# A mixture-of-experts block with streamed weights: the experts that need two passes move from places 6, 12, 18, 24 to places 3, 10, 17, 24

## The reference

```python
logits = (xt @ router_w + router_b).astype(jnp.float32)
top_v, top_e = lax.top_k(logits, TOP_K)          # TOP_K = 4, N_EXPERTS = 32
wts = jax.nn.softmax(top_v, axis=-1)
...
def expert_block(args):
    xb, e = args
    hgu = xb @ w_gate_up[e] + b_gate_up[e]       # 1024 -> 2048
    gate, up = jnp.split(hgu, 2, axis=-1)
    gate = jnp.minimum(gate, SWIGLU_LIMIT)
    up = jnp.clip(up, -SWIGLU_LIMIT, SWIGLU_LIMIT)
    act = (up + 1.0) * (gate * jax.nn.sigmoid(SWIGLU_ALPHA * gate))
    return act @ w_down[e] + b_down[e]           # 1024 -> 1024
```

## Time and profile before

| | |
|---|---|
| three runs | 1380.29, 1381.20, 1381.88 us; median 1381.2 us |
| the profiled execution | 1381.2 us, of which its span is 1379.5 us |
| PE busy | 1339.8 us (97% of the span) |
| POOL busy | 710.9 us (52%) |
| DVE, ACT busy | 412.0 us (30%), 234.7 us (17%) |
| read from memory | 483.44 MB, mean 352 GB/s |
| expert stage | first block's `gate_up` ends at 434.87 us, the last block's at 1354.10 us |

### The profile page before, as it was taken

One profiled execution on the slowest core, in us unless ns is written; L12 is line 12 of the kernel. 1 busy time (PEld: TensorE's weight loads), 2 busy tenths in 40 slices (PEclk: granted clock), 3 DMA queues, 4 the chain that ended last, 5 costly groups with the idle time before them and its releaser, 6 DMA issues.

```text
span 1379.5 us, 17459 instructions
## 1 busy us (share of the span) xinstructions
PE 1339.8 (97%) x6442; PEld 624.2 (45%) x6443; DVE 412.0 (30%) x755; ACT 234.7 (17%) x401; POOL 710.9 (52%) x425
## 2 busy tenths in 40 slices
PE   5999999999999999999999999999999999999996
PEld 2888545788743333333333333333333333333332
DVE  2160015355664331113321322312232231231222
ACT  2320004310023111111211211211211211211202
POOL 0000000000013777768777677777677776777773
PEclk9899999999999999999999999999999999999999
DMA  9735342599757999999999989999899998999995
GB/s 351 252 123 183 122 138 106 190 324 362 275 227 308 431 428 429 429 399 420 428 429 429 427 365 428 430 427 429 363 429 429 427 429 362 430 429 427 431 427 221
DMA packets 70914, 485.89 MB, mean 352 GB/s; under 512 B 7254, under 2 KB 7418, under 8 KB 45450
## 3 DMA queue, kind: packets, MB, share of 16 engines
q1 hardware_dynamic: 69490, 480.56, 85.1%
q0 software_dynamic: 1056, 3.93, 1.0%
q10 hardware_dynamic: 344, 1.07, 0.2%
HBM read 483.44 MB, written 2.10 MB: 352 GB/s over the span
## 4 chain that ended last, share of the span: by engine, by line
PE 70%; DMA 26%; DVE 1%; issue 1%; POOL 1%; SPq 1%; ACT 1%; DVEq 0%; POOLq 0%; ACTq 0%
PE bank L1600 22%; DMA landing<-in_w_gate_up 17%; PE bank L1261 15%; PE bank L1647 12%; DMA landing<-in_w_down 7%; PE bank L1270 6%; PE bank L1579 4%; PE bank L1617 2%; PE bank L1496 2%; DMA piece<-in_w_ada 1%; PE bank L1634 1%; PE bank L1544 1%; POOL gu_slot L527 1%; PE bank L1607 1%; PE bank L1630 1%
## 5 line engine op out<-in xcount | busy, mean ns | idle before, releaser
L527 POOL COPY gu_slot<-landing 128x2048 f32<-128x2048 f32 x248 | 463.0, 1898 | 196.7 <-issue 117.5
L1600 PE MATMUL bank<-gu_slot,xg 128*64 128x512 f32 x2304 | 510.7, 593 | 8.8 <-POOL gu_slot L527 7.9
L1600 PEld LDWEIGHTS bank<-gu_slot,xg 128*64 128x64 f32 x2304 | 162.4, 137 | 329.0 <-issue 295.8
L527 POOL COPY dn_slot<-landing 128x2048 f32<-128x2048 f32 x124 | 231.3, 1897 | 76.3 <-issue 55.5
L1647 PE MATMUL bank<-dn_slot,actT 128*64 128x512 f32 x1152 | 255.1, 595 | 0.0
L1647 PEld LDWEIGHTS bank<-dn_slot,actT 128*64 128x64 f32 x1152 | 79.5, 137 | 171.2 <-issue 171.2
L1261 PE MATMUL bank<-hT,piece 128*128 128x256 f32 x704 | 155.1, 382 | 0.0
L1170 DVE TENSOR_SCALAR bank<-bank 128x512 f32<-128x512 f32 x36 | 25.2, 699 | 399.2 <-PE bank L1600 399.2
L1261 PEld LDWEIGHTS bank<-hT,piece 128*128 128x128 f32 x704 | 134.5, 192 | 19.6 <-issue 1.1
L744 ACT ACTIVATE sig<-bank 128x512 f32<-128x512 f32 x36 | 21.5, 598 | 696.7 <-PE bank L1600 696.7
L1180 DVE TENSOR_TENSOR ysb<-bank,gt2q 128x512 f32<-128x512 f32 x36 | 24.9, 692 | 253.7 <-PE bank L1647 253.7
(11 more groups left out here) (323 smaller groups left out, 902.7 us busy)
## 6 DMA issues: line engine op xcount, KB each, us to landing
landing<-in_w_gate_up SPq DMA_DIRECT2D x124, 2048.0 KB, 10.7
landing<-in_w_down SPq DMA_DIRECT2D x62, 2048.0 KB, 10.7
piece<-in_w_in SPq DMA_DIRECT2D x17, 2048.0 KB, 8.7
piece<-in_w_ada SPq DMA_DIRECT2D x12, 2048.0 KB, 13.1
gu_slot<-in_w_gate_up SPq DMA_DIRECT2D x8, 1024.0 KB, 7.3
piece<-in_w_branch_a SPq DMA_DIRECT2D x2, 2048.0 KB, 9.2
dn_slot<-in_w_down SPq DMA_DIRECT2D x4, 1024.0 KB, 11.3
piece<-in_w_branch_b SPq DMA_DIRECT2D x2, 2048.0 KB, 8.7
```

Of the source, the lines that this page charges most:

```text
L527: nc.gpsimd.tensor_copy(place, landing[j // 2 % 3][:, j % 2, :]).then_inc(there, 16)
L1600: ins = M(gu_bank[u][64 * q:64 * q + 64, :], xg[:, k % 4, 64 * (k // 4):64 * (k // 4) + 64], gu_slot[k][:, cols_], start=(k == 0), stop=(k ...
```

## The change

It is one table, written by GpSimd in the first stage. Ranks 0 to 4 now stand at places 3, 10, 17, 24, 31; ranks 5 to 8 at 7, 14, 21, 28; 9 to 12 at 5, 12, 19, 26; 13 to 17 at 1, 8, 15, 22, 29; 18 to 22 at 2, 9, 16, 23, 30; 23 to 26 at 4, 11, 18, 25; 27 to 30 at 6, 13, 20, 27; rank 31 at 0. With these inputs the four doubles are at 3, 10, 17 and 24.

```diff
             at = 0
-            for first, n in ((6, 5), (3, 5), (5, 5), (2, 5), (1, 6), (4, 5), (0, 1)):
+            for first, n in ((3, 5), (7, 4), (5, 4), (1, 5), (2, 5), (4, 4), (6, 4), (0, 1)):
                 step.settle()
-                step(nc.gpsimd.iota(place_of[:, at:at + n], [[6, n]], base=first, channel_multiplier=0,
+                step(nc.gpsimd.iota(place_of[:, at:at + n], [[7, n]], base=first, channel_multiplier=0,
                                     allow_small_or_imprecise_dtypes=True), numbers_ready if first == 0 else None)
                 at += n
```

## The result

The changed kernel took 1367.73 us (median of 4 executions, 1366.56 to 1368.81) against 1381.43 us for the kernel before (median of 4, 1380.29 to 1381.88): ratio 0.9902, 95% interval 0.9885 to 0.9919. It is 13.7 us faster where 9.2 were forecast, and 1367.73 lies under the range. The profiled execution of the changed kernel took 1366.56 us with a span of 1364.9 us, 14.6 us less than the span before.

A forecast was written before the change was run, and what follows sets the result against it. Weight transfers were taken to bound the expert stage until about 600 us, TensorE after. Removed waits (-10.40) and new ones (+1.27) gave -9.1 us, the queue's side -9.5 to -10.0; with -9.2 taken, 1381.2 became 1372.0 us, range 1370.0 to 1374.5.

The forecast's parts named there:

- The first double at 3: Expert stage: a second block at place 3 builds lead for the transfers, removing the waits of places 4 to 6, -10.40 us.
- The last double: End of the expert stage: it stays at place 24, seven singles and the tail follow, nothing changes but its time.
- Six singles between doubles: Expert stage: six singles outlast the lead slightly, so places 10, 17 and 24 newly wait 0.42 us each, +1.27 us.
- The 0.42: Lateness in us of place 31 before the change, taken as the wait into places 10, 17, 24 and 31 after it.
- The check from the queue's side: SyncE's issue queue: holds behind doubles fall from 18.1 or 17.6 us to 8.1, moving the end by -10.0 or -9.5 us.
- L = 20.4 us: Expert stage: the transfers' capped lead at the place behind a double; each single uses 3.47 us, so it lasts six singles.
- A lead that is shorter behind a double met with nothing in hand: Rival, expert stage: places 9, 16 and 23 wait too, at most 3.47 us more per stretch; 1375.5 to 1382.5 us; chance 0.06.
- A shortage of buffers: Rival, places 4 to 6: three landing buffers, not transfer rate, cause the pauses, which stay; 1382.5 us, no difference; chance 0.04.
- The clock in the expert stage: Rival: TensorE without pauses from 513 us drops its clock, about 7 us per stretch; two stretches give 1386 us; chance 0.03.
- The table does what it says: Answers a rival: if doubles were not ranks 0 to 3, they would not move to 3, 10, 17; no difference; chance 0.02.
- 1381.2 - 9.2: Whole kernel: profiled execution, also the median of three runs, less the gain taken from both sums, giving 1372.0 us.
- a rival in the other direction: The slower case: TensorE's clock falls after 513 us as in the first 100 us, about 7 us per stretch; chance 0.03.

The follow-up runs named there:

- e1: Kernel before with its same placement, table written in eight pieces instead of seven: 1378.61 us against 1377.45, ratio 1.0.
- e5: Kernel before plus 16 products of constants in TensorE's pauses at the start: 1378.1 us, ratio 1.0002 to the kernel before.
- e3: Against the kernel before: first double at place 3, steps kept at six (doubles at 3, 9, 15, 21): 1378.2 us, ratio 1.0005.
- e4: Against the changed kernel: first double back at place 6, steps of seven (doubles at 6, 13, 20, 27): 1378.4 us, ratio 1.0011 to the kernel before.
- e7: Against the changed kernel: steps of eight (doubles at 3, 11, 19, 27): 1378.97 us against 1377.73 for the kernel before, ratio 1.0004.
- e8: Against the changed kernel: first double at place 2, steps of seven (doubles at 2, 9, 16, 23): 1370.62 us, ratio 0.9955 to the kernel before.
- e2: The changed kernel timed again with no edit: 1367.48 us against 1377.45 for the kernel before, ratio 0.9924.
- e10: The changed kernel timed once more with no edit, beside the one with ten added products: 1366.88 us, ratio 0.9923 to the kernel before.
- e6: Changed kernel plus 16 products of constants in TensorE's pauses at the start: 1368.4 us, ratio 0.9933 to the kernel before.
- e9: Changed kernel plus ten products of constants at the start, none behind colA: 1369.33 us against 1377.62 for the kernel before, ratio 0.9948.

## Why the prediction was right and wrong

**The mechanism and the size of the gain in the expert stage: right.** The first double at 3 takes the 10.40 us of places 4 to 6 (measured: all three at 25.93). The step "The last double" was right too. The term "Six singles between doubles" was sized at 3 x 0.42 = 1.27 us and measured 0.24 + 0.23 + 0.11 = 0.58, and place 31 waits 0.28 instead of 0.42; place 3 is met 0.09 later. That is 10.40 - 0.58 + 0.14 - 0.09 = 9.87, and the trace shows 9.83. The 0.42 was one reading: with the same table place 31 is 0.19 late in e1 and 0.17 in e5, and in the five traces of the changed table the waits run from 0.06 to 0.38. The check from the queue's side, -9.5 to -10.0, was the better of the two sums. L = 20.4 us, drawn from one wait of 0.42, stood up to every placement: with it, and with the changed kernel's measured stage as the base, e3, e4, e7 and e8 were forecast at 919, 919.4, 919.6 and 911.9 us and came at 919.15, 919.56, 919.92 and 911.83.

**The rivals.** A lead that is shorter behind a double met with nothing in hand: places 9, 16 and 23 show no wait. A shortage of buffers: the pauses of places 4 to 6 are gone with the same three buffers, and come back wherever a stretch of singles outlasts the lead (e3, e7), so they are the transfer rate's. That the buffers set how long the lead can get was read from GpSimd's and SyncE's waits; no run has another number of them. The clock in the expert stage stays at 1.00. The table does what it says.

**The step that failed is the base of the last sum, the 1381.2 in "1381.2 - 9.2".** I took the profiled execution's first stage as given, a term of zero in the difference, and the spread of three runs (0.8 us either way) as the whole spread. The runs showed a first stage that ended 4.41 us earlier (430.46 for 434.87), and a kernel before whose median over 59 more executions is 1377.65; from that base the same 9.2 would have given 1368.45. The trace held the warning: in the earlier trace rows the first 100 us have a granted clock of 0.93, which I used only for a rival in the other direction. What happens ahead of L1340 sets the end of the first block: in all twelve traces it follows 363.36 to 363.38 us behind L1340's start. By the mean clock of the first 70 us as the profile gives it:

| kernel | mean clock, 0 to 70 us | L1340 starts | first block ends |
|---|---|---|---|
| e7 | 0.88 | 72.50 | 435.87 |
| before | 0.90 | 71.51 | 434.87 |
| e1, e3 | 0.93, 0.93 | 69.33, 69.25 | 432.69, 432.63 |
| after, e2, e4 | 0.98, 0.98, 0.98 | 67.08, 67.18, 67.14 | 430.46, 430.55, 430.50 |
| e8 | 0.95 | 67.04 | 430.41 |
| e10 | 0.98 | 68.17 | 431.55 |
| e5, e6, e9 (added products) | 0.98, 0.98, 0.98 | 68.77, 68.70, 68.50 | 432.13, 432.07, 431.88 |

e4, with an unlucky table and a lucky start, shows that the 430.5 are not the change's, and so do the medians: the median time less the stage is 457.5 to 459.5 us in all eight runs without added products (after 458.3, e4 458.8, e10 457.5) and 458.2 to 458.5 for the kernel before beside them, but 462.2 for it in the first comparison. The mean is a rough guide, and the last three rows don't follow it. e10 has its one dip between 50 and 60 us, in the second 64 products of L1261, where it cost 1.7 us. The kernels with added products wait for the late piece. And the profile's clock misses time at the lower level before about 20 us: the kernel after reads 1.00 from 10 to 20 us, though its sixteen products of L1249 at 16.99 took 3.59 us where sixteen at 22.41 took 1.92; e8, with 2.76 us for the same products, reads 0.89. The times of equal products are the safer measure.

Over 59 executions timed beside the experiments the kernel before has a median of 1377.65 (1375.73 to 1381.16). Of these, the 18 with a mean clock of 0.997 have a median of 1376.55, and the 6 with 0.993 have 1380.69; between them the order isn't strict (0.994: 1378.30, 0.995: 1378.87). Measured beside each other in the two groups that ran the changed kernel again, the change is worth 10.0 and 10.7 us (ratios 0.9924 and 0.9923), and 9.7 in the pair with added products. So of the 13.7 us some 10 are the change's, and the rest is that the kernel before was slow in the first comparison: its four executions took 1380.29 to 1381.88, while the changed kernel's took what it took later. Only 7 of the 59 reach 1380.29, so four of four is hardly the same luck. In the one of the four that was traced it is TensorE's clock at the start; for the other three no clock is on record.

That the clock makes the difference between traces is shown by the equal products that take longer in one of them, with nothing gained or lost behind L1340. What sets the length of the stretch at 1.2 GHz, and what made the first four executions slow together, stays open. The Trainium skill, TensorE: Matmul & The Clock Gate, section What's actually happening, says that the default state is throttled and that activity releases the throttle. The traces agree in part: the first sixteen products of L1249, behind TensorE's pause at the start, took 3.32 to 3.64 us, and with added products ahead of them 1.92 to 2.15; and in most traces a clock under 1.00 lies between 20 and 40 us, in and right behind the pauses and the one-column products (L1289), and from 70 us to 1340 us it is 1.00 in all. But in the kernel before, e7 and e10 the windows from 50 to 60 us show 0.83 to 0.86 in the middle of dense products, which that rule doesn't explain and no run here does.

## What to carry to other kernels

When transfers are a little slower than the work on them and now and then a piece of work is used twice, count the lead: what a double gives, what the buffers can hold of it, what each single takes. The best spacing is the one at which the lead just reaches zero at the next double and again at the end; start the first one where the starting lead ends. This held for even steps and one set of buffers. A change of the spacing or of the start alone can show nothing and the two together all of it.

Before a sum is made against a profiled execution, look whether its stages outside the change are typical: a granted clock under 1.00 in the first windows is time that the next execution may not have. Time the kernel before again beside the changed one: here its first four executions lay 3.8 us over the median of the next 59.

## What was unexpected of the hardware

The same kernel spreads over 5 us, 0.4% of its time, and between traces nearly all of the difference outside the expert stage lies ahead of L1340, in the first 73 us. One stretch at 1.2 GHz over dense products cost 1.7 us (64 products of L1261: 15.77 for 14.08), and the slowest start here (e7, 435.87) is 5.5 us behind the best (e8, 430.41). Filling TensorE's pauses ahead of them gained no time: the spread was 2.3 us in one kernel (e5) and 5.5 in another (e9), and the fourth weight piece landed some 1.3 us later.
